# First block's attentions in pairs of heads, with dense products, splits of weights and the start of the output product moved into their steps

## The chip, the cores and the metric

One NeuronCore of one Trainium2 chip runs the whole program in one launch. The metric is the device time in microseconds (us), median of several executions. TensorE (PE) multiplies, VectorE (DVE) and ScalarE (ACT) do elementwise work, GpSimd (POOL) does small scalar work and some loads, and SyncE (SP) issues the loads of weights. Each engine works through its own queue in order, and engines wait for each other by semaphores.

## The reference, cut to what matters

Two transformer blocks run one after the other on 256 tokens of width 1024, all in float32. The first has four layers: mixers A, B, C, A. The change touches this block alone.

```
for i in range(4):                        # kinds A, B, C, A
    if kind == A:   # 16 query heads, 4 key/value heads of 64, window 128, a sink logit per head
        h = softmax(mask(rope(q) @ rope(k).T / 8), sink) @ v @ w_o + b_o
    elif kind == B: # 16 heads, three dilation groups, each its own q, k, v (9 x 1024 columns)
        h = merge of the three groups' outputs by their softmax sums @ w_o
    else:           # C: with 256 tokens there is one block, so it is causal attention, 16 heads
        h = softmax(causal(rope(q) @ rope(k).T / 8)) @ v @ w_o
    x = layer_norm(ALPHA * x + h)
    x = layer_norm(ALPHA * x + swiglu(x, w_gate_up[i], w_down[i]))
```

## The kernel before, in words

The 256 tokens are two row tiles of 128 (t = 0, 1). Every dense product is done in three passes: activations and weights are each split into a high part, rounded to fp32r, and the remainder (`xt_hi`, `xt_lo`, `whi`, `wlo`), and hi*hi, lo*hi and hi*lo are summed in PSUM. Weights come in chunks of 1024 rows x 512 columns (2 MB), loaded by SP in two halves of 512 rows into one of three slots (`raw`, `SLOTS = 3`). ACT writes `whi` (L969), then DVE writes `wlo` (L1270), each in halves. A chunk costs PE 2 tiles x 8 k-steps x 3 = 48 matmuls of 128x512. A k-step is three matmuls, here and below. Chunk w + 3 may be loaded and split only when chunk w's product is over: `sp.wait_ge(lin_done, fin[w - SLOTS])`, and the same wait on ACT.

The program is a list of stages (`add`), and each engine walks through the same list, doing its own share of each stage: so the order of the list is the order of every queue. `linear` is a dense product of one chunk, `pair` one of two chunks, `rope` the rotation on DVE, `turn` the transposition of q or k by PE (L1932) with ACT's copy back to SBUF (L1077), `split` the transposition of the attention's output `r` (L1992) with its hi part by ACT (L990) and lo part by DVE (L1292), `renorm` the output product with the residual, the layer norm and the first transposition of its result.

An attention (`attention`) is a loop over units. In A and C a unit is one head with both row tiles, 16 units, in B one head of one row tile, 16 units for each half of the heads. A unit costs: scores on PE (L2092, two units at once, each on half of the array's rows), on DVE the masked row minimum of the negated scores (L1637, `maxima`), on ACT the exponentials with their sums (L1094, `exps`), on PE the transposition (L2104, `turned`), the copy back to SBUF by DVE (L1654, for B partly by ACT, L1105), values on PE (L2121), on ACT the scaled evacuation (L1113). Scores go to four PSUM banks (S0, S1, L0, L1). Inside the loops of the first block no chunk is split. One late `linear` or `turn` (`behind`) is placed as a whole near the loop's start. The second block's attentions run with a `fill`: a dense product cut into portions behind each unit, and there the half splits of the next weights are done at the end of a unit's step.

After the loop PE transposes the whole of `r` in four groups (`split`), then multiplies tile 0 with both chunks of w_o, then tile 1. In `renorm`, DVE finishes the split of chunk w + 2 between the residuals of the two halves of tile 0; PE transposes tile 0's normed rows (`turn_rows`) after 12 of tile 1's 16 k-steps, and the FFN's first product follows 4 k-steps later.

## Time and profile before

| | us |
|---|---|
| median of 3 runs | 2468.96 (2465.37 to 2470.01) |
| the profiled execution: its own time | 2470.61 |
| the profiled execution: its span | 2468.8 |
| PE busy | 2400.2 (97%) |
| DVE busy | 1511.0 (61%) |
| ACT busy | 1171.0 (47%) |

The span runs from the first to the last instruction. Matmuls are pipelined, and the length shown for one (0.39 us for a 128x512) is longer than the distance from its start to the next start: the distance between starts is what one costs in a row of them. The idle time in brackets names what ended it.

### The profile page before, as it was taken

The numbers are of one execution on the slowest core, as the hardware profiler recorded it, in microseconds if no ns is written. First come the engines' busy times: TensorE is split into PE (matmuls) and PEld (weight loads), VectorE is DVE, ScalarE is ACT, GpSimd is POOL, SyncE is SP. The second block draws the span as 40 slices with busy tenths as digits, with TensorE's granted clock in tenths as the row PEclk, the third lists the DMA queues.
The fourth block names the chain that finished last, engine by engine and source line by source line (L and its number), as shares of the span: only waits on it lengthen the run. The fifth ranks groups of instructions, "written<-read, shape, count | busy, mean of one in ns | idle before, by whom it ended". The sixth has DMA issues, their size and how long they took to land.

```text
span 2468.8 us, 32201 instructions
## 1 busy us (share of the span) xinstructions
PE 2400.2 (97%) x13024; PEld 1990.6 (81%) x13024; DVE 1511.0 (61%) x2130; ACT 1171.0 (47%) x1609; POOL 107.9 (4%) x138
## 2 busy tenths in 40 slices
PE   6999999999999999999999999999999999999999
PEld 5788887877888778886888878887888878987887
DVE  6754655456546475467655676676555676677553
ACT  3644355455443564436434355573434455564442
POOL 2100000001000010000100100000100000000000
PEclk9999999999999999999999999999999999999999
DMA  6355343343553445543654335353754434445642
GB/s 234 137 205 204 137 176 132 137 171 128 199 202 137 174 149 207 205 157 121 249 195 167 119 137 205 120 205 128 273 197 161 146 109 178 146 173 180 234 172 85
DMA packets 263122, 419.00 MB, mean 170 GB/s; under 512 B 12192, under 2 KB 149408, under 8 KB 262976
## 3 DMA queue, kind: packets, MB, share of 16 engines
q1 hardware_dynamic: 258112, 400.15, 45.8%
q0 software_dynamic: 4864, 16.80, 1.9%
q8 instruction: 105, 1.72, 0.3%
q14 instruction: 41, 0.34, 0.0%
HBM read 415.86 MB, written 1.05 MB: 169 GB/s over the span
## 4 chain that ended last, share of the span: by engine, by line
PE 87%; DVE 6%; ACT 3%; issue 2%; DMA 1%; POOL 1%; SPq 0%; DVEq 0%; ACTq 0%; POOLq 0%
PE bank_L L1979 39%; PE bank_L L1963 18%; PE bank_S L2183 7%; PE bank_O L2183 7%; PE bank_L L1960 3%; PE bank_O L2121 2%; DVE wlo L1270 2%; PE bank_T L2104 1%; PE bank_T L2166 1%; PE bank_S L1963 1%; PE bank_S L2092 1%; ACT whi L969 1%; PE bank_O L1963 1%; PE bank_T L1920 1%; PE bank_T L1992 1%
## 5 line engine op out<-in xcount | busy, mean ns | idle before, releaser
L1270 DVE TENSOR_TENSOR wlo<-raw,whi 128x2048 fp32r<-128x2048 f32 (+1 forms) x332 | 712.3, 2170 | 286.7 <-ACT whi L969 286.2
L969 ACT ACTIVATE whi<-raw 128x2048 fp32r<-128x2048 f32 (+1 forms) x332 | 593.8, 1817 | 61.0 <-DMA raw<-in_w_in 21.2
L1979 PE MATMUL bank_L<-whi,xt_hi 128*128 128x512 f32 x1440 | 572.1, 397 | 9.2 <-DVE wlo L1270 7.5
L1979 PE MATMUL bank_L<-wlo,xt_hi 128*128 128x512 f32 x1440 | 564.3, 392 | 0.0
L1979 PE MATMUL bank_L<-whi,xt_lo 128*128 128x512 f32 x1440 | 563.4, 391 | 0.0
L1979 PEld LDWEIGHTS bank_L<-whi,xt_hi 128*128 128x128 f32 x1440 | 272.0, 189 | 64.8 <-issue 8.6
L1151 ACT ACTIVATE tok<-bank_L 128x256 f32<-128x256 f32 x132 | 50.7, 384 | 566.3 <-PE bank_L L1979 566.3
L1979 PEld LDWEIGHTS bank_L<-wlo,xt_hi 128*128 128x128 f32 x1440 | 271.6, 189 | 57.6
L1963 PE MATMUL bank_L<-whi,xt_hi 128*128 128x512 f32 (+1 forms) x800 | 314.5, 393 | 2.9 <-DVE wlo L1270 2.9
L1979 PEld LDWEIGHTS bank_L<-whi,xt_lo 128*128 128x128 f32 x1440 | 272.2, 189 | 53.7
L1963 PE MATMUL bank_L<-wlo,xt_hi 128*128 128x512 f32 (+1 forms) x800 | 308.7, 386 | 0.0
L1963 PE MATMUL bank_L<-whi,xt_lo 128*128 128x512 f32 (+1 forms) x800 | 308.2, 385 | 0.0
L1691 DVE TENSOR_TENSOR tok<-tok,bank_L 128x256 f32<-128x256 f32 x132 | 55.6, 421 | 301.9 <-ACT tok L1151 301.6
L1963 PEld LDWEIGHTS bank_L<-whi,xt_hi 128*128 128x128 f32 x800 | 150.6, 188 | 34.6 <-issue 5.7
L1963 PEld LDWEIGHTS bank_L<-wlo,xt_hi 128*128 128x128 f32 x800 | 150.4, 188 | 30.5
L1963 PEld LDWEIGHTS bank_L<-whi,xt_lo 128*128 128x128 f32 x800 | 150.7, 188 | 28.1
L1684 DVE TENSOR_TENSOR dlo<-draw,dhi 128x1024 fp32r<-128x1024 f32 x132 | 155.5, 1219 | 4.1 <-ACT dhi L1145 3.4
L1145 ACT ACTIVATE dhi<-draw 128x1024 fp32r<-128x1024 f32 x132 | 131.8, 1050 | 0.0
L1007 ACT ACTIVATE tok<-bank_L 128x512 f32<-128x512 f32 x68 | 40.7, 598 | 186.6 <-PE bank_L L1963 139.2
L1094 ACT ACTIVATE sm<-sm,small 128x256 f32<-128x256 f32 (+5 forms) x176 | 89.7, 512 | 54.3 <-DVE small L1637 34.4
L2183 PE MATMUL bank_O<-dhi,yt_hi 128*128 128x512 f32 x264 | 104.0, 394 | 0.0
L2183 PE MATMUL bank_S<-dhi,yt_hi 128*128 128x512 f32 x264 | 103.5, 392 | 0.0
(309 smaller groups left out, 3141.8 us busy)
## 6 DMA issues: line engine op xcount, KB each, us to landing
raw<-in_w_gate_up SPq DMA_DIRECT2D x176, 512.0 KB, 5.7
raw<-in_w_in SPq DMA_DIRECT2D x72, 1024.0 KB, 6.3
draw<-in_w_down SPq DMA_DIRECT2D x44, 1024.0 KB, 6.2
raw<-in_ffn_w_up SPq DMA_DIRECT2D x88, 512.0 KB, 5.7
raw<-in_b_w_qkv SPq DMA_DIRECT2D x36, 1024.0 KB, 7.0
draw<-in_ffn_w_down SPq DMA_DIRECT2D x22, 1024.0 KB, 5.7
raw<-in_w_lift SPq DMA_DIRECT2D x32, 512.0 KB, 4.4
raw<-in_a_w_qkv SPq DMA_DIRECT2D x12, 1024.0 KB, 8.1
```

Of the source, the lines that this page charges most:

```text
L969: act.activation(wide(whi, w, nkc, ncols)[:, ks, :], wide(raw, w, nkc, ncols)[:, ks, :], ACT.Copy) \
L1094: ins = act.activation(st["ps"][:, k % 3, q], st["ps"][:, k % 3, q], ACT.Exp, bias=nb[:, k % 4, row:row + 1], scale=-1.0, accum_out=ls[:, ...
L1145: act.activation(dhi[d % 2, k][:, :], draw[:, d % 2, k, :], ACT.Copy).then_inc(dhi_done, 1)
L1151: act.activation(silu_g[:, o % 2, :], banks[LB[o % 2]][:, 0:FN], ACT.Silu).then_inc(silu_done, 1)
L1270: dve.tensor_tensor(wide(wlo, w, nkc, ncols)[:, ks, :], wide(raw, w, nkc, ncols)[:, ks, :], wide(whi, w, nkc, ncols)[:, ks, :].bitcast(F32 ...
L1684: dve.tensor_tensor(dlo[:, d % 2, k, :], draw[:, d % 2, k, :], dhi[d % 2, k][:, :].bitcast(F32), ALU.subtract).then_inc(dlo_done, 1)
L1691: dve.tensor_tensor(hid[:, j % 2, t, :], silu_g[:, o % 2, :], banks[LB[o % 2]][:, FN:2 * FN], ALU.mult) \
L1960: mm = pe.matmul(banks[name][:, o], ww[:, kk, c0:c0 + P], xx[:, kk, :], start=(kk == 0 and q == 0), stop=(kk == nkc - 1 and q == 2))
L1963: mm = pe.matmul(banks[name][:, 0:st["ncols"]], xx[:, kk, t * P:(t + 1) * P], ww[:, kk, :], start=(kk == 0 and q == 0), stop=(kk == nkc - ...
L1979: mm = pe.matmul(banks[bank][:, :], xx[:, k, t * P:(t + 1) * P], ww[:, k, :], start=(k == 0 and q == 0), stop=(k == KC - 1 and q == 2))
L2121: mm = pe.matmul(banks[name][half, row * u["dv"]:(row + 1) * u["dv"]], pts[:, k % 2, c * P + half.start:c * P + half.stop], v, start=(q == ...
L2183: mm = pe.matmul(banks[ACC[t][h]][:, :], yy[:, 2 * b + k, t * P:(t + 1) * P], ww, start=(j == 0 and k == 0 and q == 0), stop=(j == FJ - 1 ...
```

## The change

1. The first block's attentions become a new stage `paired`: a step handles a pair of units. PE's step i is: scores of pair i, values of pair i - 2, transpositions of pair i - 1, then portions of dense products, a turn of queries or keys, a group of transpositions of `r`, and a part of the output product. Two steps of drain follow the last pair.
2. Late products are cut into portions over steps: A the second half of q's chunk, B the last v chunk and (first half of heads) the next half's first q and k chunks, C three chunks (q, k, v of heads 8 to 15).
3. The half splits of the next chunks, w_o's among them, are done at given steps (`splits`), by ACT and DVE at the end of their own step; so are rotations (`ropes`), turns, and the groups of `r` (`groups`).
4. The first 16 of the output product's 32 k-steps run inside the loop (`parts`). Tile 0 goes to L0 and L1, tile 1 to S0 and S1. `renorm` has the rest.
5. Scores have two banks in A and C (S0, S1), four in B (S0, S1, L1, O1); B has one bank for values (O0) and one for its dense portions (L0).
6. A chunk of w_o frees its first half for loading and splitting as soon as its k-steps 0 to 3 are through (`part_done`).

```diff
+        LATE_PARTS = {5: [(0, 0, 0, 2)], 6: [(0, 1, 0, 2)], 7: [(0, 0, 2, 4), (0, 1, 2, 4)], 8: [(1, 0, 0, 4)],
+                      9: [(0, 0, 4, 6), (0, 1, 4, 6)]}
...
                 # A
+                part(q1, 0, 5)
                 turn(tks[1], q_ok, qT[:, 0:4], by=BY)
                 first = (turn_done, n["turn"])
+                part(q1, 5, 8)
+                q1_rope, ok = rope(heads(tk), 8, 0, q1_in, inside=True)
+                q1_turn = turn_inside(tk, ok, qT[:, 4:8], by=BY)
...
+                att = paired(pairs, first, SB, OB, lambda q, w: (2 * (q % 2) + w) * 386, lambda q, w: w * 384,
+                             fill=[(q1, 0, 2)], ropes={2: q1_rope}, turns={3: q1_turn},
+                             splits={1: (w1, (0,)), 2: (w1, (1,)), 3: (w1 + 1, (0,)), 4: (w1 + 1, (1,))},
+                             groups={4: [(0, 2)], 6: [(1, 4)], 8: [(2, 6)]}, parts=LATE_PARTS, turned=hv)
...
                 # B, first half of the heads
+                        paired(pairs, first, fill=[(st, 0, 2), (early_[0], 2, 5.5), (early_[1], 5.5, 9)],
+                               splits={0: (w1, (0, 1)), 3: (w1 + 1, (0,)), 4: (w1 + 1, (1,)), 7: (w1 + 2, (0,)), 8: (w1 + 2, (1,))},
+                               **banked)
                 # B, second half
+                        att = paired(pairs, first, fill=[(st, 0, 2)],
+                                     splits={1: (w1, (0,)), 2: (w1, (1,)), 4: (w1 + 1, (0,)), 5: (w1 + 1, (1,))},
+                                     groups={2: [(0, 0)], 3: [(1, 0)], 6: [(2, 4)]}, turned=hv,
+                                     parts={4: [(0, 0, 0, 2)], 5: [(0, 0, 2, 4)], 7: [(0, 0, 4, 6)],
+                                            8: [(0, 1, 0, 4), (1, 0, 0, 2)], 9: [(0, 1, 4, 6), (1, 0, 2, 4)]}, **banked)
...
                 # C: pair of chunks q0, k0; then v0; then
+                part(late[0], 0, 3)
+                att = paired(pairs, first, SB, OB, lambda q, w: (2 * (q % 2) + w) * 384, lambda q, w: w * 384,
+                             fill=[(late[0], 0, 1.4), (late[1], 1.4, 2.8), (late[2], 2.8, 5)], ropes=ropes_, turns=turns_,
+                             splits={0: (w1 + 1, (0, 1)), 2: (w1 + 2, (0, 1)), 4: (w1 + 3, (0,)), 5: (w1 + 3, (1,)),
+                                     6: (w1 + 4, (0, 1))},
+                             groups={5: [(0, 2)], 6: [(1, 4)], 8: [(2, 6)]}, parts=LATE_PARTS, turned=hv)
...
+        def freed(w, h):
+            if h == 0 and w - SLOTS in early:
+                return (part_done, early[w - SLOTS])
+            return (lin_done, fin[w - SLOTS])
...
                 # ACT
+                    for i in range(len(J) + 3):
+                        for late in st["fill"]:
+                            for t in ended(late, i - 1):
+                                if late["evac"] == "act":
+                                    evacuated(late, t, late["into"][t])
...
+                        if i < len(J):
+                            pair_exps(i)
+                        if 1 <= i <= len(J):
+                            pair_copies(i - 1)
+                        if i >= 2:
+                            pair_evacuate(i - 2)
+                        if i in st["splits"]:
+                            split_hi(*st["splits"][i])
+                        if i in st["turns"]:
+                            heads_hi(st["turns"][i])
+                        for g, _ in st["groups"].get(i, ()):
+                            group_hi(st["rows"], g)
...
                 # DVE, after the biased evacuations of the same form
+                        if i < len(J):
+                            pair_maxima(i)
+                        if 1 <= i <= len(J):
+                            pair_copies(i - 1)
+                            pair_reciprocal(i - 1)
+                        if i in st["ropes"]:
+                            rotated(st["ropes"][i])
+                        if i in st["splits"]:
+                            split_lo(*st["splits"][i])
+                        for g, _ in st["groups"].get(i, ()):
+                            group_lo(st["rows"], g)
...
                 # DVE, renorm
+                        if st["begun"]:
+                            group_lo(st["begun"]["rows"], 3)
+                            split_upto(w + 2)
                         add_residual(st, 0, 0)
...
                 # PE, renorm
+                    if st["begun"]:
+                        turn_group(st["begun"]["rows"], 3)
+                        output(st, 1, 1, 0, 4)
+                        output(st, 0, 0, 6, 8)
+                        output(st, 0, 1, 6, 8)
+                        output(st, 1, 0, 4, 8)
+                        output(st, 1, 1, 4, 6)
+                        turn_rows(st, 0)
+                        output(st, 1, 1, 6, 8)
...
                 # PE
+                    for i in range(len(J) + 2):
+                        if i < len(J):
+                            pair_scores(i)
+                        if i >= 2:
+                            pair_values(i - 2)
+                        if 1 <= i <= len(J):
+                            pair_turned(i - 1)
+                        todo = [(late, q) for late in st["fill"] for q in range(*portion(late, i))]
+                        for late, q in todo[:len(todo) // 2]:
+                            product(late, q, q + 1)
+                        if i in st["turns"]:
+                            turn_heads(st["turns"][i])
+                        for late, q in todo[len(todo) // 2:]:
+                            product(late, q, q + 1)
+                        for g, _ in st["groups"].get(i, ()):
+                            turn_group(st["rows"], g)
+                        for t, h, k0, k1 in st["parts"].get(i, ()) if st["parts"] else ():
+                            output(st["out"], t, h, k0, k1)
```

`portion` spreads a product's k-steps evenly over the steps a to b that it is given. `output(st, t, h, k0, k1)` does k-steps k0 to k1 of tile t with half h of w_o. A part `(t, h, k0, k1)` and a group `(g, pairs)` are read the same way; the group waits until that many pairs are evacuated.

## Rows read from the trace of the kernel before

**Rows 1.** The page: span and instructions; busy us, share and instructions of each engine.
```profile
span 2468.8 us, 32201 instructions
PE 2400.2 (97%) x13024; PEld 1990.6 (81%) x13024; DVE 1511.0 (61%) x2130; ACT 1171.0 (47%) x1609; POOL 107.9 (4%) x138
```
**Rows 2.** Windows of the first layer: stretch, length, busy us (instructions) PE PEld DVE ACT POOL, clock, DMA.
```profile
46.10:57.10 11.00, 11.00 (x51) 9.06 (x50) 8.49 (x11) 6.03 (x6) 0.00 (x0) 1.00 0.53 192
57.10:88.35 31.25, 27.17 (x338) 19.65 (x336) 24.70 (x121) 25.11 (x103) 1.08 (x2) 1.00 0.26 85
88.35:111.30 22.95, 22.95 (x108) 19.12 (x107) 18.12 (x17) 10.28 (x9) 1.67 (x2) 1.00 0.29 98
```
**Rows 3.** Timeline of PE (start us, us): first layer, from one pair to the next.
```profile
78.00 0.57 PE L2121 MATMUL bank_O<-arena,pts 128*64 128x64 f32 x12
78.50 0.93 PE L2092 MATMUL bank_L<-arena 64*128 64x128 f32 x8
79.36 0.55 PE L2104 MATMUL bank_T<-ident,sm 128*128 128x128 f32 x3
```
**Rows 4.** Timeline of PE, second layer: values, then scores of the wide kind.
```profile
555.98 0.92 PE L2121 MATMUL bank_O<-arena,pts 128*64 128x64 f32 x24
556.83 0.48 PE L2092 MATMUL bank_L<-arena 64*128 64x256 f32 x1
```
**Rows 5.** The chain in order of time (start, us): one chunk's product.
```profile
380.60 10.92 PE bank_L L1963 x48
```
**Rows 6.** Timeline of DVE and ACT, second block's attention: one step with a half split.
```profile
2084.42 0.28 DVE L1637 CUSTOM_DVE_ANT_0 sm<-bank_S,sm 128x128 f32<-128x128 f32 x1
2085.09 0.40 ACT L1094 ACTIVATE sm<-sm,small 128x128 f32<-128x128 f32 x1 [2.92 <-DVE small L1637]
2087.07 0.49 ACT L1113 ACTIVATE arena<-bank_O,small 128x64 f32<-128x64 f32 x2
2087.46 1.90 ACT L969 ACTIVATE whi<-raw 128x2048 fp32r<-128x2048 f32 x1
2089.39 2.29 DVE L1270 TENSOR_TENSOR wlo<-raw,whi 128x2048 fp32r<-128x2048 f32 x1 [2.72 <-ACT whi L969]
2091.60 0.28 DVE L1637 CUSTOM_DVE_ANT_0 sm<-bank_S,sm 128x128 f32<-128x128 f32 x1
```
**Rows 7.** Timeline of DVE, first layer: the masked minimum with sink, the next copy.
```profile
77.90 0.35 DVE L1637 CUSTOM_DVE_ANT_0 sm<-bank_S,masks,sk 128x128 f32<-128x128 f32 x1
78.58 0.55 DVE L1654 COPY pts<-bank_T 128x384 f32<-128x384 f32 x1
```
**Rows 8.** Timeline, first layer's norm of tile 0, and the turn of its rows.
```profile
101.19 0.68 DVE L1304 SCALAR_TENSOR_TENSOR r<-x,bank_L 128x512 f32<-128x512 f32 x1
104.81 1.29 DVE L1339 SCALAR_TENSOR_TENSOR x<-x,small,arena 128x1024 f32<-128x1024 f32 x1 [0.55 <-POOL small L934]
107.50 1.03 PE L1920 MATMUL bank_T<-ident,x 128*128 128x128 f32 x8
```
**Rows 9.** Timeline of PE: ends of the stretches in the second and third layer.
```profile
391.45 0.94 PE L2092 MATMUL bank_S<-arena 64*128 64x128 f32 x12
457.64 1.03 PE L1932 MATMUL bank_T<-ident,tok 128*128 128x128 f32 x8
528.44 0.94 PE L2092 MATMUL bank_S<-arena 64*128 64x128 f32 x12
599.73 1.04 PE L1920 MATMUL bank_T<-ident,x 128*128 128x128 f32 x8
812.82 1.03 PE L1932 MATMUL bank_T<-ident,tok 128*128 128x128 f32 x8
909.92 1.03 PE L1920 MATMUL bank_T<-ident,x 128*128 128x128 f32 x8
```
**Rows 10.** Windows at the end of the third layer's attention, and right behind it.
```profile
882.00:888.40 6.40, 4.27 (x63) 3.28 (x64) 3.01 (x10) 4.41 (x18) 1.13 (x2) 1.00 0.12 41
888.40:891.80 3.40, 3.40 (x13) 2.84 (x13) 1.72 (x3) 2.39 (x3) 0.00 (x0) 0.54 0.72 239
```

More of the change, by code:

```diff
@@ L261, in renorm @@
                         finishes(n["w"] + half, t, t == T - 1)
+                if begun:
+                    begun["out"] = st
+                    for half in range(2):
+                        n["part"] += 1
+                        early[n["w"] + half] = n["part"]
                 n["w"] += 2
@@ L363, in attention @@
[L363 to L366 removed]
+                        u["pieces"].append((row, off, width, mask, products))
+                        off += width
+                u["cols"] = off
+                n["seg"] += 1
                 n["ttr"] += len(u["pieces"])
                 n["p"] += 1
[L369 removed]
@@ L370, in attention @@
[L370 to L377 removed]
+                n["tp"] += 1
@@ L481, in build @@
-                o_is = attention(units, [(turn_done, n["turn"]), (dev, n["dev"])], first, behind, in_twos=True)
+                part(q1, 5, 8)
+                q1_rope, ok = rope(heads(tk), 8, 0, q1_in, inside=True)
+                q1_turn = turn_inside(tk, ok, qT[:, 4:8], by=BY)
+                q1_ok = (turn_done, n["turn"])
+                hv = halves(r)
+                pairs = []
+                for h0 in range(0, 16, 2):
+                    two = []
+                    for h in (h0, h0 + 1):
+                        kv, rows = h // 4, []
+                        for t in range(T):
+                            m, nk = causal(1, t)
+                            rows.append(([(m, [(head_ap(qT, h, t * P, t * P + P),
+                                                kT[HD * (h % 2):HD * (h % 2) + HD, kv, 0:nk], nk)])],
+                                         [vv[:, s, kv * HD:kv * HD + HD] for s in range(nk // P)],
+                                         r[:, t, h * HD:h * HD + HD]))
+                        two.append(dict(rows=rows, sink=(j, h), needs=q1_ok if h >= 8 else None,
+                                        needs_v=v_ok if h == 0 else None))
+                    pairs.append(two)
@@ L564, in build @@
-                o_is = attention(units, [(aev, n["aev"])], (turn_done, n["turn"]), [st], in_twos=True)
+                        ropes_[2 + which], ok = rope(c_heads(dst), 8, 0, done, inside=True)
+                        turns_[2 + which] = turn_inside(dst, ok, (qT, kT)[which][:, 4:8], by=(BY, 1.0)[which])
+                qk_ok = (turn_done, n["turn"])
+                v_ok.append((aev, n["aev"]))
+                part(late[0], 0, 3)
+                hv = halves(r)
+                pairs = []
@@ L2128, in _ @@
                     for i in range(len(U) + 3):
-                        if i == st["lead"]:
-                            for late in st["behind"]:
-                                (turn_heads if late["kind"] == "turn" else product)(late)
+                        if i == 2:
                             for s_, v in st["ready"]:
```

580 lines of the change are left out of this document (379 added, 201 removed).

## The prediction

> **What bounds the kernel now.** I read the page first: PE is busy 2400.2 of 2468.8 us and DVE 1511.0 [rows 1], so time can be won only where PE idles or is slow. Busy time misleads for short matmuls, whose shown lengths overlap, so next I read the timeline of PE by distances between starts. A chunk's 48 matmuls take 10.92 us [rows 5], so a k-step costs 0.68 and dense stretches have no gaps to win. Then the windows of the first layer [rows 2]: q's second chunk fills 46.10 to 57.10, then comes the attention with the transposition of its output (31.25 us, DVE 24.70 and ACT 25.11 busy), then 32 k-steps of w_o with one turn of rows (22.95, gapless). In the attention a pair's scores take 0.86 us (78.50 to 79.36), a head's values 0.50 at most [rows 3], a head's three transpositions about 0.33 (eight show 1.03 with their pipeline's tail [rows 9]). Eight pairs are 8 x (0.86 + 0.66 + 0.70) = 17.8 us (0.70 for both heads' values, 24 matmuls: 0.85 with the gap behind them [rows 4]), the turn of q 0.9, the transpositions of r 1.7: 20.4 of 31.25. So some 11 us of PE lie idle in each A layer. That is the room of the change; B's and C's attentions leave less.
>
> The question is whether PE, now given dense work in those gaps, will find the other two engines in time. For that I read DVE and ACT in the second block's attention, which already splits weights inside its steps [rows 6]. A step runs there as one chain through both engines: first minimum 2084.42, exponentials 2085.09 to 2087.07, an evacuation, ACT's hi part at 2087.46, DVE's lo part only at 2089.39 (it idled 2.72 us for it), and the next minimum at 2091.60. Nothing overlaps: 7.18 us for two units and one half split, though DVE's own work in it, by its instructions, is about 4.5 us. The same order stands in the new loop: ACT does the hi part behind its exponentials, DVE waits for it with its lo part, and the next pair's minimum is queued behind that.
>
> **What the change costs, layer A (twice).** I walk from 46.10, q's second chunk, to 111.30, the FFN's first product: 65.2 us before.
> - Before the loop: 8 k-steps 5.4, the turn of q 0.9 with its gaps: 6.6.
> - Step 0: scores 0.9, 4 k-steps 2.7, then scores of pair 1; its minimum starts 4.9 us into the loop.
> - Steps 1 to 4 have one half split each. The step of rows 6 plus 0.4 (both heads are evacuated before the hi part), plus 0.2 (the minimum with its sink column takes 0.73 a head [rows 7], against 0.55), less 0.2 (the second head's minimum no longer waits behind a copy): 7.6 each, 30.4 together. PE has for them: step 1 4.8, step 2 2.6, step 3 3.6, step 4 3.3, together 14.3. The dense portions are in the wrong steps: q's end with step 1, w_o's first k-steps come in step 5, since a group of r needs its heads first. So 16 us of PE idle here. The rotation and the copies on DVE are hidden under ACT's hi part. Not hidden: the bias of q's last tile 0.7, and the lo part of the first group 0.7.
> - Then the minimum of pair 5 (1.5), and PE sets the pace. Per pair 2.6 (scores 0.9, values 0.9, transpositions 0.8, gaps of about 0.1 to 0.2 between kinds as in rows 3) with groups at 0.6 and parts at 0.68 a k-step: step 6 from its scores on 4.6, 7 5.3, 8 5.0, 9 3.6, gaps 0.4: 18.9.
> - Loop: 4.9 + 30.4 + 1.4 + 1.5 + 18.9 = 57.1.
> - `renorm` has 16 k-steps, 10.9 us, where it had 21.8. But the cover of the norm goes with them. DVE now does the whole split of chunk w + 2 ahead of the first residual: group turned and its hi part 0.6 + 0.7, ACT's first hi half 1.9 more, two lo halves 2.2 each: 7.8. Then residual and statistics of the first half 1.4, and from the second residual (101.19) to the end of the norm (104.81 + 1.29) 4.9 [rows 8]: 14.1. PE reaches `turn_rows` at 10.1 and stalls 4.0. From there 2.5 to the FFN (turn 1.1, 2 k-steps 1.4): 16.7, against 22.95 - 10.9 = 12.05.
> - Sum: 6.6 + 57.1 + 16.7 = 80.4, so **+15.2 for each A**, +30.4. For layer 4 I take the same.
>
> **C.** From 813.86 (after the turn at 812.82) to 913.7 (the turn at 909.92 plus 3.8, as 107.50 to 111.30 in the first layer) [rows 2, 8, 9]: 99.8 us. After: v0 10.9, turn 0.9, 3 k-steps and gaps 2.3: 14.1. Steps 0 to 4 carry 45 k-steps and keep PE busy, so the splits in them are hidden: 7.1, 8.8, 11.2, 8.5, 8.4 = 44.0. Step 5: scores 0.9, values, transpositions and group to 3.2, then a wait for the lo half and group 0 until 8.9 (the chain of 7.4 without sink, a late evacuation of v, the group's lo), part 1.4: 10.3. Step 6 splits two halves: PE has 3.3 and then waits until 8.5 for w_o's second chunk, part 1.4: 9.9. Steps 7 to 9: 5.3, 5.0, 3.6 = 13.9. Loop 78.1. `renorm` 16.7. Sum 108.9: **+9.1**.
>
> **B.** Wide scores (12 of 256 columns, 6 distances of 0.21) cost 1.5, values of 24 matmuls 0.85 [rows 4], so a narrow and a wide pair take PE 2.4 for scores, 2.5 for values, 2.7 for transpositions and 0.4 of gaps: 8.0. First half, 391.45 to 457.64 [rows 9], 66.2: eight pairs 32.0 and 48 k-steps 32.6 are 64.6. The portions all go through L0: where a product passes from one tile to the next in the middle of a step, PE must wait for an evacuation that ACT does only at the start of its next step, behind exponentials and hi part. That is so in steps 3, 5 and 7: 0.8, 0.8, 1.7, further gaps 0.3. Then the rotation of q waits behind the last split, 1.8: 70.0, **+3.8**. Second half, 528.44 to 603.5 (599.73 + 3.8), 75.0: PE's ten steps are 6.3, 8.1, 4.3, 4.5, 5.0, 5.2, 4.3, 5.2, 6.9, 4.3: 54.1; chains with splits or group parts in steps 2 to 6 add about 9.3 (in steps 2, 3 and 4 a T bank is held by a group until its lo part; in 6 the copy of pair 5 is behind a lo half): 63.4, plus 16.7: **+5.1**.
>
> **Bounds of what no row shows.** A step of the new loop is not in the trace. Below, the nearest row is the old pair at 2.83 us of both DVE and PE plus a lo half 2.2, 5.0, if ACT ran ahead; above, 7.18 with everything extra added and nothing taken off, 8.2. I take 7.6, since the order of waits is that of rows 6. The ends make A -10 or +2 each. The early free half slot: ACT and SP get chunk w + 3 some 5 us sooner; nothing waits for it in the rows of the first layer (the window 88.35 to 111.30 has PE busy throughout), so 0, at most 1 us won for each of four layers; it cannot cost, since the issues are the same. DMA, SP and POOL have the same work; only POOL's gains rows are asked for at the same event and needed 9 us later, as `centre` comes earlier: 0. The reciprocals fall from two to one a pair, 0.07 each, inside DVE's time.
>
> Sum: 30.4 + 9.1 + 3.8 + 5.1 = +48.4, on the profiled execution's own 2470.6: 2519.0. The median of the runs is 1.6 lower, so **2517 us**.
>
> **Rivals.**
> 1. *Each step takes only what its busiest engine has to do.* ACT and DVE hide in each other, A's ten steps become 3.6, 4.7, 6.6, 4.7, 5.4, 3.6, 4.0, 5.0, 4.5, 3.4: 45.5. For it: in the old loop both were 80% busy and still overlapped [rows 2]. Against: rows 6. A 6.6 + 45.5 + 16.7 = 68.8, +3.6 each; C -2; B first half -2, second -2. Total +1: 2470.
> 2. *PE's work alone sets the time*, splits and norm covered. A's loop is 8 x 2.6 for the pairs, 1.0 for the turn, 1.8 for three groups, 24 k-steps 16.3 and gaps 0.5: 40.4, and 6.6 + 40.4 + 12.5 = 59.5, -5.7 each; C 14.1 + 67.1 + 12.5, -6.1; B -1.6 and 54.1 + 12.5, -8.4: -27.5, so 2441. For it: PE is the bound everywhere else. Against: PE has 14.3 us for steps 1 to 4 while DVE and ACT have 9 and 7.2 for the splits alone. It decides if a split step costs under about 3.6.
> 3. *The clock.* Right after a stretch of 6.40 us with PE busy 4.27, the grant was 0.54 over 3.40 us with PE fully busy, that is the 1.2 GHz level [rows 10]: 1.7 us lost. In none of A's steps 1 to 4 is PE busy for a larger share than in that stretch. If the grant falls two or three times in each loop, with dense k-steps in it, 5 loops x 1 to 2 more x 1.7 = about +12 over my forecast: 2529.
>
> The Trainium skill ("TensorE: Matmul & The Clock Gate", section "HAM oscillation — how this bites in real kernels") says that small idles between bursts of matmuls can make the gate drop and recover over and over; the trace shows one such drop behind C's loop, so the rule speaks for rival 3 and for my sign, and against a layout with thin steps. By the rule the time would be rival 3's.
>
> **How the numbers follow.** My forecast has 0.50 (its own range 2500 to 2533), rival 3 0.12, rival 1 0.16, rival 2 and its neighbours down from 2455 0.22. A run tells 0.2% (5 us) from no change. Rival 1 lies around that: of its 0.16 a third each way. Faster 0.22 + 0.05 = 0.27, same 0.05, slower 0.62 + 0.06 = 0.68. The range leaves out most of rival 2 and little above: 2450 to 2535.
>
> **What would show it.** In A's steps 1 to 4 the distance between first minima is 7 to 8 us, with DVE's lo part put down to waiting 2 us for ACT's hi part; PE waits before the scores of pairs 3 to 5 and before the first part. In all four `renorm` PE waits about 4 us for `turn_rows`, on DVE's x. In C two waits of 5 us, in steps 5 and 6, on wlo or xt_lo. In B short waits for L0 on ACT. I am wrong if split steps in A are under 6 us, or if PE's turn of rows comes without a wait.

## The result and the profile after

The changed kernel takes **2532.81 us** (median of 4 runs, 2530.61 to 2535.77); the kernel before, on the same chip, 2469.49 (2465.37 to 2472.14). The ratio is 1.0259 (95% interval 1.0240 to 1.0278): slower by 63.3 us. The profiled spans are 2532.8 and 2468.8 [rows 1], 64.0 apart.

First the head of the page of the changed kernel, to hold against [rows 1]:

```profile
span 2532.8 us, 32056 instructions
PE 2415.0 (95%) x13024; PEld 1997.9 (79%) x13024; DVE 1509.8 (60%) x2090; ACT 1169.4 (46%) x1609; POOL 107.9 (4%) x138
PE 83%; DVE 8%; ACT 4%; issue 3%; DMA 1%; POOL 1%; SPq 0%; DVEq 0%; ACTq 0%; POOLq 0%
```

The work is nearly the same; the third line, the chain that ended last, has PE at 83% where the page of the kernel before has 87%, and more of DVE (8% against 6%) and ACT (4% against 3%). Where the time went is best read from one landmark that every layer has, the turn of rows (the first transposition of tile 0's normed rows), in PE's timeline (start, length, instruction, idle before it and its releaser):

```profile
124.68 1.09 PE L2155 MATMUL bank_T<-ident,x 128*128 128x128 f32 x8 [3.58 <-DVE x L1524]
630.00 1.09 PE L2155 MATMUL bank_T<-ident,x 128*128 128x128 f32 x8 [3.55 <-DVE x L1524]
954.96 1.37 PE L2155 MATMUL bank_T<-ident,x 128*128 128x128 f32 x8 [3.56 <-DVE x L1524]
1250.17 1.97 PE L2155 MATMUL bank_T<-ident,x 128*128 128x128 f32 x8 [3.55 <-DVE x L1524]
```

Before they started at 107.50, 599.73, 909.92 and 1187.30 [rows 8, 9], the fourth read from the same view. So layer 1 (A) lost 17.2 us, B 13.1, C 14.8, layer 4 (A) 17.8: 62.9. What follows each turn has to be counted too. These windows run from it to the same turn of tile 1 (start and end, length, busy us of PE, PEld, DVE, ACT and POOL, granted clock, DMA):

```profile
124.68:136.53 11.85, 11.85 (x57) 9.90 (x57) 11.10 (x12) 6.36 (x6) 4.21 (x4) 1.00 0.93 340
630.00:643.45 13.45, 13.45 (x57) 11.02 (x57) 11.19 (x12) 6.36 (x6) 4.72 (x4) 0.87 0.84 309
954.96:968.41 13.45, 13.45 (x56) 11.13 (x57) 11.29 (x12) 6.47 (x6) 4.36 (x4) 0.87 0.85 304
1250.17:1264.78 14.61, 14.61 (x56) 12.14 (x57) 11.29 (x12) 6.46 (x6) 4.92 (x5) 0.80 0.80 291
```

Before, this took 13.13 to 13.16 us, with two k-steps more in it. With them gone it takes 11.85 in layer 1, but in the other three layers part of it runs at half clock (the lower level, 1.2 GHz), which costs 1.6, 1.6 and 2.8 us: 6.0 together. Taken from tile 1's turn to tile 1's turn (120.65, 612.86, 923.08 and 1200.44 before), the layers lost 15.9, 14.7, 14.7 and 19.0 us, 64.3 in all. The rest of the program is no longer than before.

Now layer 1's loop, from DVE's timeline. The four `wlo` are the half splits' lo parts, the others the first minimum of pairs 2 to 5:

```profile
61.30 2.29 DVE L1454 TENSOR_TENSOR wlo<-raw,whi 128x2048 fp32r<-128x2048 f32 x1 [1.98 <-ACT whi L1104]
64.18 0.35 DVE L1868 CUSTOM_DVE_ANT_0 sm<-bank_S,masks,sk 128x128 f32<-128x128 f32 x1
69.47 2.29 DVE L1454 TENSOR_TENSOR wlo<-raw,whi 128x2048 fp32r<-128x2048 f32 x1 [1.45 <-ACT whi L1104]
71.75 0.35 DVE L1868 CUSTOM_DVE_ANT_0 sm<-bank_S,masks,sk 128x128 f32<-128x128 f32 x1
77.04 2.29 DVE L1454 TENSOR_TENSOR wlo<-raw,whi 128x2048 fp32r<-128x2048 f32 x1 [2.77 <-ACT whi L1104]
79.71 0.35 DVE L1868 CUSTOM_DVE_ANT_0 sm<-bank_S,masks,sk 128x128 f32<-128x128 f32 x1 [0.30 <-PE bank_S L2342]
85.01 2.29 DVE L1454 TENSOR_TENSOR wlo<-raw,whi 128x2048 fp32r<-128x2048 f32 x1 [1.83 <-ACT whi L1104]
87.89 0.35 DVE L1868 CUSTOM_DVE_ANT_0 sm<-bank_S,masks,sk 128x128 f32<-128x128 f32 x1
```

The minima of pairs 2 to 5 are 7.57, 7.96 and 8.18 us apart, and each lo part waited 1.4 to 2.8 us for ACT's hi part, as in [rows 6]. ACT idles in turn: its next exponentials wait for the minimum behind that lo part:

```profile
64.97 0.40 ACT L1237 ACTIVATE sm<-sm,small 128x129 f32<-128x129 f32 x1 [3.70 <-DVE small L1868]
67.53 1.91 ACT L1104 ACTIVATE whi<-raw 128x2048 fp32r<-128x2048 f32 x1
72.54 0.40 ACT L1237 ACTIVATE sm<-sm,small 128x129 f32<-128x129 f32 x1 [3.11 <-DVE small L1868]
```

What PE, the engine that ought to set the pace, waits for in that loop (timeline again):

```profile
65.83 1.65 PE L2342 MATMUL bank_S<-arena 64*128 64x128 f32 x8 [3.00 <-DVE small L1868]
73.87 1.94 PE L2167 MATMUL bank_T<-ident,tok 128*128 128x128 f32 x8 [3.44 <-DVE pts L1883]
78.03 1.65 PE L2342 MATMUL bank_S<-arena 64*128 64x128 f32 x8 [2.23 <-ACT arena L1126]
88.05 0.52 PE L2354 MATMUL bank_T<-ident,sm 128*128 128x128 f32 x3 [2.46 <-DVE xt_lo L1477]
```

And C, steps 5 and 6, with a lone wait for the first k-steps of each of w_o's chunks:

```profile
910.61 0.77 PE L2214 MATMUL bank_L<-whi,xt_hi 128*128 128x512 f32 x1 [5.44 <-issue]
913.44 1.50 PE L2342 MATMUL bank_S<-arena 64*128 64x128 f32 x8
922.59 0.77 PE L2214 MATMUL bank_L<-whi,xt_hi 128*128 128x512 f32 x1 [4.88 <-DVE wlo L1454]
925.42 1.65 PE L2342 MATMUL bank_S<-arena 64*128 64x128 f32 x8
927.00 1.50 PE L2375 MATMUL bank_O<-arena,pts 128*64 128x64 f32 x24
```

The two k-steps that begin at 910.61 and at 922.59 last 2.83 us each, against 1.36 for two k-steps at the rate of [rows 5]; the scores are 1.50 and 1.65 long, against 0.93 in the steps ahead of the wait, and the values behind the second 1.50 against 0.92: half clock, right behind each wait. The windows 900 to 915 us and 915 to 930 us have a granted clock of 0.77.

### The profile page after: what moved, and what is told of

It reads as the page before. It is cut to its first block, busy times and chain, and to the rows that moved or that the text cites. A ratio compares the mean times of both kernels' runs of the same rounds, so it can differ in the third digit from the quotient of the medians.

```text
span 2532.8 us, 32056 instructions
## 1 busy us (share of the span) xinstructions
PE 2415.0 (95%) x13024; PEld 1997.9 (79%) x13024; DVE 1509.8 (60%) x2090; ACT 1169.4 (46%) x1609; POOL 107.9 (4%) x138
## 4 chain that ended last, share of the span: by engine, by line
PE 83%; DVE 8%; ACT 4%; issue 3%; DMA 1%; POOL 1%; SPq 0%; DVEq 0%; ACTq 0%; POOLq 0%
PE bank_L L2214 36%; PE bank_L L2198 17%; PE bank_S L2507 7%; PE bank_O L2507 7%; PE bank_L L2195 3%; DVE wlo L1454 3%; ACT whi L1104 2%; PE bank_S L2342 1%; PE bank_T L2490 1%; PE bank_S L2198 1%; PE bank_O L2375 1%; PE bank_T L2354 1%; PE bank_T L2155 1%; PE bank_O L2198 1%; PE bank_T L2243 1%
## 5 line engine op out<-in xcount | busy, mean ns | idle before, releaser
L2214 PE MATMUL bank_L<-whi,xt_hi 128*128 128x512 f32 x1376 | 548.2, 398 | 17.0 <-DVE wlo L1454 10.1
L2214 PE MATMUL bank_L<-wlo,xt_hi 128*128 128x512 f32 x1376 | 539.7, 392 | 0.0
L2214 PE MATMUL bank_L<-whi,xt_lo 128*128 128x512 f32 x1376 | 538.5, 391 | 0.0
L2214 PEld LDWEIGHTS bank_L<-whi,xt_hi 128*128 128x128 f32 x1376 | 260.2, 189 | 70.4 <-issue 16.8
L2214 PEld LDWEIGHTS bank_L<-wlo,xt_hi 128*128 128x128 f32 x1376 | 259.9, 189 | 55.8
L2214 PEld LDWEIGHTS bank_L<-whi,xt_lo 128*128 128x128 f32 x1376 | 260.5, 189 | 51.2
L2198 PEld LDWEIGHTS bank_L<-whi,xt_hi 128*128 128x128 f32 x800 | 150.4, 188 | 39.2 <-issue 6.4
L2198 PEld LDWEIGHTS bank_L<-wlo,xt_hi 128*128 128x128 f32 x800 | 150.3, 188 | 31.0
L2198 PEld LDWEIGHTS bank_L<-whi,xt_lo 128*128 128x128 f32 x800 | 150.6, 188 | 27.6
L1237 ACT ACTIVATE sm<-sm,small 128x129 f32<-128x129 f32 (+5 forms) x128 | 67.3, 527 | 109.6 <-DVE small L1868 82.1
```

What stands on the lines that cost most here:

```text
L1237: ins = act.activation(smflat[:, q], smflat[:, q], ACT.Exp, bias=nb2[:, c:c + 1], scale=-1.0, accum_out=ls2[:, c:c + 1])
L2198: mm = pe.matmul(banks[name][:, 0:st["ncols"]], xx[:, kk, t * P:(t + 1) * P], ww[:, kk, :], start=(kk == 0 and q == 0), stop=(kk == nkc - ...
L2214: mm = pe.matmul(banks[bank][:, :], xx[:, k, t * P:(t + 1) * P], ww[:, k, :], start=(k == 0 and q == 0), stop=(k == KC - 1 and q == 2))
```

## The experiments

Every run was measured beside the kernel before on the same chip, so the ratios are the fair comparison. The groups e1 to e4, e5 to e8, e9 to e11 and e12 ran on four different chips; the median of the kernel before was 2468.6 to 2470.1 us on them, so a difference of 1.5 us between groups says nothing. The starts of the four turns of rows (PE, us) tell the layers apart:

| kernel | median us | ratio to before (95%) | layer 1 | B | C | layer 4 | PE's wait before them |
|---|---|---|---|---|---|---|---|
| before | 2469 to 2470 | | 107.50 | 599.73 | 909.92 | 1187.30 | 0 |
| changed | 2532.81 | 1.0259 (1.0240 to 1.0278) | 124.68 | 630.00 | 954.96 | 1250.17 | 3.6 |
| e1 hi first | 2497.59 | 1.0117 (1.0102 to 1.0132) | 115.69 | 609.61 | 927.40 | 1213.48 | 3.6 |
| e2 FFN's split inside | 2521.37 | 1.0211 (1.0195 to 1.0226) | 122.18 | 628.89 | 949.46 | 1240.67 | 0.9 |
| e3 parts outside | 2526.86 | 1.0238 (1.0222 to 1.0253) | 122.89 | 631.56 | 950.12 | 1244.77 | 0 |
| e4 keep busy | 2530.21 | 1.0250 (1.0233 to 1.0267) | 123.24 | 630.95 | 953.68 | 1248.74 | 3.6 |
| e5 = e1 + e2 | 2481.12 | 1.0047 (1.0032 to 1.0062) | 114.41 | 604.09 | 918.80 | 1201.26 | 0.9 |
| e6 spread | 2471.88 | 1.0007 (0.9998 to 1.0017) | 111.45 | 601.02 | 909.27 | 1189.67 | 0.9 |
| e7 no early half | 2532.63 | 1.0261 (1.0244 to 1.0279) | 124.01 | 631.67 | 954.45 | 1249.65 | 3.6 |
| e8 copy shared | 2473.74 | 1.0017 (1.0008 to 1.0027) | 111.97 | 601.90 | 910.72 | 1193.37 | 0.9 |
| e9 later | 2468.05 | 0.9994 (0.9985 to 1.0003) | 109.49 | 599.16 | 907.43 | 1186.81 | 0.9 |
| e10 parts first | 2468.82 | 0.9997 (0.9988 to 1.0005) | 112.07 | 601.78 | 910.88 | 1189.07 | 0.9 |
| e11 lo lags | 2518.92 | 1.0202 (1.0186 to 1.0217) | 120.38 | 619.21 | 945.33 | 1236.27 | 3.6 |
| e12 = e9, parts outside | 2495.55 | 1.0106 (1.0089 to 1.0123) | 117.11 | 612.14 | 926.84 | 1213.16 | 0 |

My theory was that of the prediction: in a step with a half split one chain runs through both engines, minimum, exponentials, hi part (ACT), lo part (DVE), next minimum. Its rivals: the clock, PE's own pace with the cover of the norm gone, and the parts placed in the wrong steps.

**e1: ACT's hi part ahead of its exponentials.** Only the order in ACT's queue changes.

```diff
+                        if i in st["splits"]:
+                            split_hi(*st["splits"][i])
                         if i < len(J):
                             pair_exps(i)
...
-                        if i in st["splits"]:
-                            split_hi(*st["splits"][i])
```

> The changed kernel with one edit: in a step of the paired loop ACT does the hi part of the half split before the exponentials of its pair, not behind the evacuation. Chain theory (split steps are one chain minimum, exponentials, evacuation, hi part, lo part): DVE no longer waits for the hi part, so a split step of the first layer falls from 7.6 to 8.2 us to about DVE's own work, 4.7 to 6.6; each A layer gains about 9 us, C about 6 (its waits in steps 5 and 6 shrink), B about 6; total about 30 less than 2532.8, so about 2503. Rival, PE work and the norm's wait decide: the loops hardly change, under 8 us less, 2525 or more. Rival, the clock: the gain is the chain's and the clock's together, and the granted clock goes back above 0.99.

Measured 2497.59, 35.2 less than the changed kernel, more than half of the whole loss, by the place of one piece of ACT's work in its queue. DVE's lo parts no longer wait:

```profile
59.00 2.26 DVE L1454 TENSOR_TENSOR wlo<-raw,whi 128x2048 fp32r<-128x2048 f32 x1
61.84 0.35 DVE L1868 CUSTOM_DVE_ANT_0 sm<-bank_S,masks,sk 128x128 f32<-128x128 f32 x1
65.59 2.29 DVE L1454 TENSOR_TENSOR wlo<-raw,whi 128x2048 fp32r<-128x2048 f32 x1
67.87 0.34 DVE L1868 CUSTOM_DVE_ANT_0 sm<-bank_S,masks,sk 128x128 f32<-128x128 f32 x1
70.31 2.26 DVE L1454 TENSOR_TENSOR wlo<-raw,whi 128x2048 fp32r<-128x2048 f32 x1
```

The minima of pairs 2 to 5 are now 6.0, 6.2 and 6.4 us apart, where they were 7.6 to 8.2. By the traces all of the gain lies in the loops: 8.8 us in layer 1, 3.0 and 10.0 in the two halves of B, 7.2 in C, 8.9 in layer 4. That ACT's order costs about this much is shown. How much of it is the clock's is not: the grant rose from 0.983 to 0.992, as the rival of the clock had said.

**e2: the FFN's chunk split in the loop's last steps.** It covers the norm's wait. The edit is shown for A; B and C have the same.

```diff
-                             splits={..., 4: (w1 + 1, (1,))},
+                             splits={..., 4: (w1 + 1, (1,)), 8: (w1 + 2, (0,)), 9: (w1 + 2, (1,))},
```

> The changed kernel with one edit: chunk w + 2 (the FFN's first) is split in steps 8 and 9 of the loops of all four layers instead of ahead of the first residual. Theory of the lost cover (DVE comes to the residuals about 4 us late because of that split): PE's wait before the turn of the normed rows, 3.55 to 3.6 us in each layer, falls to about 1, so 4 x 2.6 = 10 us less, 2522. Rival, the wait is the norm's own chain (residual, statistics, POOL, norm): it stays over 3 us and the time over 2530.

Measured 2521.37: 11.4 less, with the wait before the turn of rows down from 3.6 to 0.9 in all four layers (4 x 2.7 = 10.8). That the two sums are so near is partly luck. The half clock behind the turns went as well (11.85 to 11.87 us from turn to turn in all four layers, 6.0 less), and in B a new wait came in, in the output product:

```profile
620.90 0.50 PE L2216 MATMUL bank_L<-whi,xt_hi 128*128 128x512 f32 x1 [2.00 <-DVE xt_lo L1479]
```

By layers, to tile 1's turn, e2 is 2.5, 0.2, 4.4 and 5.2 us faster than the changed kernel.

**e3: parts of the output product outside.** All 32 k-steps come after the loop, in B and C too, tile 0's first and tile 1's last four behind the turn of rows; splits and groups stay inside.

```diff
-                             groups={4: [(0, 2)], 6: [(1, 4)], 8: [(2, 6)]}, parts=LATE_PARTS, turned=hv)
+                             groups={4: [(0, 2)], 6: [(1, 4)], 8: [(2, 6)]}, parts={}, turned=hv)
```

> The changed kernel with the 16 k-steps of w_o taken out of the loops and put back behind them, tile 0 before tile 1; splits, groups and fills stay. If the parts inside fill idle time of PE they are worth up to 10.9 us a layer and this is 2560 or more. My theory: in the loops' second half the parts themselves set PE's pace, so outside they cost the same 10.9, while the norm gets its cover back (3.6 us a layer) and the waits of parts for lo halves in C (5.4 and 4.9 us) go; so about 4 x 3 to 20 us less, 2510 to 2522.

Measured 2526.86, 6 less, where my theory had 11 to 23 less: a miss. The sign holds: in the changed kernel the parts inside bring nothing. The traces say why. Without them the four loops are 8.1, 5.4, 12.0 and 8.3 us shorter, 33.7 together, while the same 64 k-steps cost 43.7 us behind the loops (0.683 each). So inside they did fill some 10 us of idle time. That was lost again to the wait before each turn of rows (4 x 3.6, gone in e3) and to the 6.0 us of half clock behind the turns (gone too: 13.13 to 13.15 us from turn to turn). Some 4 us come back ahead of the edited loops of B and layer 4; I did not track these to a place. PE's waits in A's steps 2 to 4 stay much as they are; in C the two lone waits of 5.44 and 4.88 become waits for a T bank of 3.30 and 3.62, each with one of about 1 us behind it.

**e4: PE kept busy.** Steps 2 and 3 of both A loops get 24 extra matmuls of 128x512 into a free bank; their result is not used.

> The changed kernel with 24 extra 128x512 matmuls into an unused bank in steps 2 and 3 of both A layers, where PE waits for DVE; they add 5.4 us of PE work in each A loop and leave the result alone. Chain theory: the work is hidden, the granted clock stays at its upper level in A's loops, and each A layer gets 0 to 2 us shorter: 2529 to 2533. Rival, the fallen clock costs much in these loops: each A layer gains over 4 us, 2525 or less. If PE set the pace there, it would be 10.8 us longer: 2543.

Measured 2530.21, no slower. The clock did change. The same stretch by windows (PE, PEld, DVE, ACT and POOL busy, granted clock, DMA), the changed kernel first:

```profile
60.00:92.00 32.00, 20.39 (x180) 15.09 (x178) 21.92 (x65) 18.79 (x55) 0.00 (x0) 0.68 0.20 66
```

and with PE kept busy:

```profile
60.00:92.00 32.00, 23.20 (x233) 17.45 (x232) 22.98 (x73) 19.55 (x56) 0.00 (x0) 0.95 0.21 67
```

The grant rose from 0.68 to 0.95 and 24 matmuls came in free. Layer 1's turn of rows came 1.4 us earlier, but in e7 below, which leaves this loop as it is, it came 0.7 earlier with a grant of 0.79; and behind e4's turn the clock fell where it had not in the changed kernel, so tile 1's turn is at 136.70 against 136.53. So in A's thin steps most of the half clock falls on time in which PE waits for DVE anyway. The clock is a sign of the waits there, not their cause. For C, where dense parts stand right behind the waits, no run raised the clock alone.

**e5: e1 and e2 together.**

> Both edits together: ACT's hi part ahead of its exponentials in every paired step, and chunk w + 2 split in steps 8 and 9 of the loops. Theory: the two remove different waits (the chain inside the steps 1 to 6, and the turn of rows behind the splits in the output product). Alone they gave -35.2 and -11.4 us against the changed kernel's 2532.8. If they add: 2486, the wait before each turn of rows 0.9 us, and the turn of layer 1 near 113. Rival: steps 8 and 9 are full once the chain is gone, so the splits there are paid in full (about 2 x 2 us more in each of four loops): 2495 or more, no better than the first edit alone.

Measured 2481.12, 51.7 less; the parts alone had 35.2 + 11.4 = 46.6. They add, and 5 us more. The step from e1 to e5 is 16.5 us, where the wait was 4 x 2.7 = 10.7. The rest is the clock: behind a wait of 3.6 us PE takes 13.40 to 13.46 us from tile 0's turn to tile 1's in all four layers of e1, behind one of 0.9 it takes 11.84 to 11.87 in e5, 6.2 us less together. Part of the 5 us over the sum is that e2 alone had the wait of 2.00 us in B's output product, which e5 has not.

**e6: spread over the steps.** In A one half is split ahead of the loop and none in step 2, where the rotation is; in C each first part comes one step later.

```diff
                 part(q1, 0, 5)
+                add("ahead_half", w=n["w"])
                 turn(tks[1], q_ok, qT[:, 0:4], by=BY)
...
-                             splits={1: (w1, (0,)), 2: (w1, (1,)), 3: (w1 + 1, (0,)), 4: (w1 + 1, (1,)),
+                             splits={1: (w1, (1,)), 3: (w1 + 1, (0,)), 5: (w1 + 1, (1,)),
...
+        C_PARTS = {6: [(0, 0, 0, 2)], 7: [(0, 1, 0, 2)], 8: [(0, 0, 2, 4), (0, 1, 2, 4)],
+                   9: [(1, 0, 0, 4), (0, 0, 4, 6), (0, 1, 4, 6)]}
```

> The edits of e5_both, and besides: in both A layers the first half of w_o's first chunk is split ahead of the loop, in the middle of q's second product, where ACT stands idle 1.7 us before the turn of q (47.7 to 49.4) and DVE 3.3 us (48.7 to 52.0); the other three halves in steps 1, 3 and 5, so none in step 2 with the rotation; in C every first part one step later. In the kernel with ACT's hi part first DVE was busy 8.77 of 8.80 us between 63.5 and 72.3. Theory: DVE's load in steps 1 to 3 now sets A's time (its lo part 2.2 and the rotation), so the wait of 3.9 us before the turn of q goes, and C's waits of 2.7 and 2.1 us: 2 x 3 + 3 under e5_both, about 2477 to 2479. Rival: loads set it (the half is not there at 47.7, ACT waits for it and the turn of q starts late): no gain, e5_both's time or 1 to 3 us over it.

Measured 2471.88, 9.2 less than e5 and not to be told from the kernel before, and better than the 2477 to 2479 that I expected. C went from 314.7 us (turn to turn) to 308.3, twice what I had given it. In layer 1 PE's wait before the turn of q fell from 3.9 to 1.7.

**e7: the early free half slot undone.**

```diff
-            if h == 0 and w - SLOTS in early:
-                return (part_done, early[w - SLOTS])
             return (lin_done, fin[w - SLOTS])
```

> The changed kernel with the early freeing of half a slot undone: chunk w + 3 is loaded and split only when the whole of w_o's chunk w is through. Theory: nothing waits for that half, 0 us, 2532 to 2534. Rival: DVE's and ACT's half splits in the output product start earlier by it, and ahead of the norm; without it the wait before each turn of rows grows by some 2 us: 2540 or more.

Measured 2532.63, against 2532.81: nothing.

**e8: half of DVE's copies on ACT.**

```diff
-                    ..., [q > 0 for q in range(len(u["turns"]))]
+                    ..., [q > 0 or (w == 1 and len(u["turns"]) == 1) for q in range(len(u["turns"]))]
```

> The edits of e6_spread, and in A and C the copy of the second head's transposed probabilities (one of two copies of 128x384 in a step, about 0.5 us) on ACT and not on DVE. Theory: DVE is the busier of the two in A's steps, so 0.5 us comes off each step that DVE still sets, four to five steps in each A, one or two in C: 2 to 5 us under e6_spread. Rival: ACT's copy comes behind its exponentials and with them PE's values wait longer: 0 to 5 us over e6_spread.

Measured 2473.74, 1.9 over e6, with intervals that overlap: no gain. The theory that DVE's load still sets A's steps falls. Layer 1 is 0.5 later and layer 4's loop 1.9 longer. Where PE had waited 1.7 on DVE's copy before the turn of q, it now waits 0.9 on DVE's and then, in the middle of the turn, 1.7 on ACT's, as the waits of that layer's loop say (total, number, longest):

```profile
PE bank_T L2177 <- ACT pts L1255: 1.7, 1, 1.7
```

**e9: the second chunk's halves in steps 4 and 6.**

```diff
-                             splits={1: (w1, (1,)), 3: (w1 + 1, (0,)), 5: (w1 + 1, (1,)),
+                             splits={1: (w1, (1,)), 4: (w1 + 1, (0,)), 6: (w1 + 1, (1,)),
```

> As e6_spread, but in both A layers the halves of w_o's second chunk are split in steps 4 and 6, where e6_spread had 3 and 5. In e6_spread PE waits in these loops 1.7 us before the turn of q (step 3, on DVE's copies) and 1.8 us before the scores behind it. Theory: with no split in steps 2 and 3 the first falls to about 0.5, and DVE reaches pair 4 sooner; the lo part in step 6 falls where DVE has room: 1 to 2 us won in each A layer, 2468 to 2470. Rival: DVE's work in the loop is the same sum and is only waited for later (scores of pair 5, first part of w_o's second chunk in step 6): 2471 to 2473.

Measured 2468.05, 3.8 under e6, at the edge of what I expected. The intervals of the two ratios still touch (0.9985 to 1.0003 against 0.9998 to 1.0017), so the gain is likely rather than shown; the traces have it in the loops of A (2.4 and 0.9 us shorter) and none in B and C. But the wait before the turn of q stayed at 1.7, so the reason was wrong in part: what fell is the wait for a T bank before groups of r, 2.6 to 1.5 us, and the one behind the turn of q, 1.8 to 1.3, while one of 0.5 on the group's lo part came in.

**e10: parts ahead of the groups.** The two loops at the end of PE's step change places.

> As e9_later, and in every step PE does the parts of the output product ahead of the group of r's transpositions. In e6_spread PE waits for a T bank before these groups 2.6 us in each A layer, 1.0 in B, 2.0 in C, since DVE's copies still hold it. Theory: the parts cover these waits: up to 8 us won, about 4 to 6 of it kept: 2464 to 2466, below the kernel before. Rival: DVE's lo part of the group stands ahead of its next minimum and now waits for the parts (1.4 us of PE in step 6, 2.7 in step 8): as slow as e9_later or 2 to 5 us slower.

Measured 2468.82, as e9: the rival. The wait for the T bank went from 1.5 to 0.2 us in layer 1, and 0.8 came back as waits on the group's lo part; the turn of rows there came 2.6 us later than in e9, and layer 4's loop was 1.3 shorter.

**e11: DVE's lo part a step behind ACT's hi part.** ACT's order is that of the changed kernel; A and B alone.

```diff
+                        lag = 0 if len(st["fill"]) == 3 and st["rows"] else 1
-                        if i in st["splits"]:
-                            split_lo(*st["splits"][i])
+                        if i - lag in st["splits"]:
+                            split_lo(*st["splits"][i - lag])
```

> The changed kernel with ACT's order untouched (exponentials, evacuation, hi part), but DVE's lo part of every half split in A's and B's paired loops one step later than ACT's hi part, so DVE never stands waiting for it at a step's end. C as it is. This tests the mechanism from DVE's side. Theory: what cost the time was the chain hi part, then lo part, then next minimum; breaking it here gives what breaking it on ACT's side gave in A and B: that edit won 35.2 us, about 7 of it in C by the turns of rows (its C was +7.6 us on the kernel before, against +14.8), so 28 less here, 2505, with ACT's hi part still behind the exponentials. Rival: it was ACT's order itself (its hi part of 1.9 us ahead of the next exponentials), not DVE's wait: 2525 to 2533.

Measured 2518.92, 13.9 less: between the two. B's second half, scores to turn of rows, took 74.0 us against 81.9 changed and 71.9 in e1, so there DVE's wait was most of it (7.9 of 10.0). Layer 1 won 4.3 of e1's 9.0. ACT's timeline of the step with the turn of q shows the rest:

```profile
70.79 1.91 ACT L1104 ACTIVATE whi<-raw 128x2048 fp32r<-128x2048 f32 x1
72.59 1.08 ACT L1126 ACTIVATE arena<-bank_T 128x512 f32<-128x512 f32 x2
```

and DVE's minimum of pair 4 waits for it, through PE's scores:

```profile
75.41 0.35 DVE L1868 CUSTOM_DVE_ANT_0 sm<-bank_S,masks,sk 128x128 f32<-128x128 f32 x1 [3.19 <-PE bank_S L2343]
```

The hi part at a step's end stands before two kinds of things: DVE's lo part, and ACT's own next deeds, here the copy of the turned q. e11 takes away the first, e1 both. The first half of B keeps its 69.9 us in e11 (66.9 in e1), and PE its wait of 1.5 us for the rotation of q.

**e12: the parts outside again, now from e9.**

> As e9_later, with all parts of the output product taken out of the loops and put behind them, as in e3_parts_outside. In the changed kernel that made 6 us less, so the parts inside were worth nothing there. Theory: they were worth nothing because each step lasted as long as its chain through ACT and DVE, and PE did its parts in time that then came back as a wait; with the chain gone, steps 5 to 9 give PE room that the parts fill (at least one k-step of 0.7 us in each of five steps): 3 to 5 us more in each of four layers, 2480 to 2488. Rival: steps 5 to 9 have PE busy anyway, and a k-step costs the same inside and outside: within 3 us of e9_later's 2468.

Measured 2495.55, 27.5 more than e9, above what I expected, and against e3, where the same edit had *saved* 6. Layer 1's loop and what follows, in e9:

```profile
52.03:97.00 44.97, 39.03 (x391) 29.53 (x391) 36.12 (x121) 32.93 (x106) 0.06 (x1) 1.00 0.18 53
```

and with the parts outside:

```profile
52.03:97.00 44.97, 31.59 (x357) 23.72 (x356) 36.80 (x121) 33.17 (x107) 1.08 (x2) 0.96 0.15 49
```

DVE and ACT do the same in both (36.1 and 36.8, 32.9 and 33.2 us); PE does 7.4 us less in the second, and does it later. That is 7.6 us at layer 1's turn of rows; the other layers add 5.4, 6.4 and 6.9, and 1.3 is for two k-steps more behind the turn.

The chain does not explain the whole difference between e3 and e12, 34 us by the traces. In e9 the parts lengthen the four loops by 18.1 us, in the changed kernel by 33.7: these 15.6 us are the room that the mended steps give. Some 11 more are the wait before the turn of rows, which e3 still had to win (3.6 us a layer) and e12 hardly (0.9). Some 11 are the clock: e3 gets rid of the 6.0 us of half clock behind the turns, and e12 pays about 5 in the first k-steps behind its loops (granted clock 0.89, 0.92 and 0.92 from there to the turn in layer 1, C and layer 4). Less some 4 us that e3 lost ahead of its loops, that is the difference. So an edit's worth here depended on the cover of the norm and on the clock as much as on the chain. No run separates the three.

## Why the prediction was right, and where it fell short

2517 was forecast, 2532.81 measured, inside 2450 to 2535 and only 2 us below its upper end. The sum had +48.4 us, the profiled execution has +64.0. Layer by layer the forecast was +15.2, +8.9, +9.1, +15.2; by tile 1's turns the traces have +15.9, +14.7, +14.7, +19.0. (By tile 0's turns, with the two k-steps in the first term, it is +16.5, +8.9, +9.1, +15.2 against +17.2, +13.1, +14.8, +17.8.) The mechanism was right; what was too small is B's second half, and the clock, which the sum put at nothing.

- *A split step in A lasts 7.6 us.* Right: 7.57, 7.96, 8.18, with the lo part behind ACT's hi part as said; e1 and e11 show that this order is the cause. The loop of layer 1 took 58.9 (52.03 to the last group at 110.94), forecast 57.1.
- *Four waits of 4.0 before the turn of rows.* Right: 3.6, and e2 shows their cover. The half clock behind three of them, 6.0 us, was not in the sum.
- *B, first half +3.8.* Right: from its first scores to the turn of q 69.9 us against 66.2, with waits for L0 of 0.69, 0.72 and 2.04 (forecast 0.8, 0.8, 1.7) and 1.53 for the rotation (1.8).
- *B, second half +5.1.* Too small: 81.9 us from its scores to the turn of rows against 71.3, +10.6, less the 1.3 of the landmark. The mechanism is the one given; the term "chains in steps 2 to 6, about 9.3" was mis-sized: those steps took 36.0 us from the first scores of pair 2 (562.43) to those of pair 7 (598.48), 12.7 more than the 23.3 forecast as PE's own work in them. The granted clock over them was 0.89, so part of the 12.7 is the clock's. PE's longer waits there:

```profile
572.22 0.52 PE L2354 MATMUL bank_T<-ident,sm 128*128 128x128 f32 x3 [1.30 <-DVE xt_lo L1477]
574.98 1.08 PE L2243 MATMUL bank_T<-ident,r 128*128 128x128 f32 x4 [2.24 <-DVE pts L1883]
596.20 0.52 PE L2354 MATMUL bank_T<-ident,sm 128*128 128x128 f32 x3 [3.92 <-DVE pts L1883]
```

- *C +9.1.* Too small by 5.7. Steps 0 to 4 took 43.3 (forecast 44.0), and the two waits came with 5.44 and 4.88 (5.7 and 5.2). What the sum lacked is that the work behind each wait runs at half clock: 2 x 1.47 for the two parts, 0.6 and 0.7 for the scores behind them and 0.6 for the values behind the second (distances between starts), 4.8 in the loop, and 1.6 behind B's turn of rows: 6.4, less 1.3 by which the steps 0 to 4 and the two waits were shorter than forecast: 5.1 of the 5.7.
- *Rival 3, the clock,* had 0.12 and said 2529. It was forecast as an addition to my sum, and that is how it came, in C, at the end of B and behind the turns of rows of B, C and layer 4; in A's thin steps, where I looked for it, e4 shows no cost that can be told. The rule of the Trainium skill that I cited ("TensorE: Matmul & The Clock Gate", "HAM oscillation — how this bites in real kernels") says that waits between bursts of matmuls can make the gate drop before each burst, again and again; its example waits for DMA. This case's trace agrees, with waits for DVE: the grant over the whole span fell from 0.997 to 0.983. How much of the 15.6 us over the forecast is the clock's was not isolated by a run. Read from distances between starts it is 10.8 us (6.0 behind the turns of rows, 4.8 in C's loop), near the 12 that rival 3 had added; the steps 2 to 6 of B's second half have 3.4 more, clock and chain together. So my middle value missed mostly by this rival's term.
- *Rivals 1 and 2* fall for this kernel. Yet rival 1, each step what its busiest engine needs, is where e6 and e9 arrive (2470 forecast, 2471.88 and 2468.05). Its loop for A, 45.5 us, is near e9's 46.2 and 47.6. That the totals agree is partly luck: rival 1 kept a wait of 4.0 us before each turn of rows, and e9 has 0.9.
- *The early half slot, 0.* Right: e7.

Where did the expected gain go? PE's 11 idle us in each A layer were real, and with the chain mended the parts fill such time: in e9 they lengthen the four loops by 18.1 us, where they would cost 43.7 behind them. In the changed kernel this was lost again to the order of ACT's and DVE's work (35.2 in e1) and to the norm's missing cover with the half clock behind it (16.5 from e1 to e5). With both mended and the splits spread, the change comes out even with the kernel before (0.9985 to 1.0003), and no version tried beats it beyond its interval. What is left in e9's layer 1 are short waits, 1.7, 1.5, 1.3, 0.9, 0.9 and 0.5 us, of which e8 and e10 moved some and won none.

## What to carry to other kernels

Before you give a bound engine more work in its gaps, follow one step round through the other two queues: where two engines do a piece of work one behind the other at the step's end (hi, then lo), and the next step's first instruction stands behind it, the step lasts as long as their sum, whatever PE does. Put the first half of such a piece at the head of its engine's step. And do not judge one part of a change alone: the same edit, parts inside or outside, was worth -6 us in one kernel and +27 in another.

## What the runs showed of the hardware

- In these runs half clock had a price where PE had work and hardly one where it waited: raising the granted clock of 60 to 92 us from 0.68 to 0.95 by filler (and of layer 4's like stretch from 0.76 to 0.90) won 2.6 us in the whole program, with intervals that overlap, while two k-steps right behind a wait of 5 us cost 2.83 us in place of 1.36.
- The same wait did not always drop the clock. Behind the wait of 0.9 us before the turn of rows (e2, e5, e6, e8, e9, e10) the next 11.85 us ran at full clock in 24 of 24 layers. Behind the wait of 3.6 us (changed, e1, e4, e7, e11) the same work took 13.2 to 14.6 us in 15 of 20 layers, and 11.85 in the other five.
- As the waits went, the clock came back by itself: 0.983 (changed), 0.992 (e1), 0.993 (e5), 0.997 (e6, e9, and the kernel before).
- A wait of 5.44 us that the timeline puts down to "issue" was none of PE's: its twin of 4.88 one step later names DVE's wlo, and e6, which asks for both a step later and has the edits of e1 and e2, has neither (e5, with these edits alone, has 2.68 and 2.10).
